# A transformer in one kernel: gate products of the second block in three passes of high and low parts, their weights split by GpSimd

## The chip, the cores and the metric

The kernel runs on one core of one Trainium2 chip. The metric is the device time of one execution in microseconds, the median of three runs. A core has TensorE (PE, matrix products into eight banks of accumulators), VectorE (DVE), ScalarE (ACT), GpSimd (POOL) and SyncE (SP, which here only issues transfers).

## The reference, cut to what matters

The input of 256 tokens by 1024 goes through two blocks of two layers each, all in float32. The second block, the one that matters here, has in each of its two layers a mixer:

```
p_swa, p_rwkv, p_fox, p_dsa, p_gate = split_cols(x @ w_in, IN_GROUPS)
o_swa, o_rwkv, o_fox, o_dsa = (four branches: two kinds of attention, a recurrent
                               one in chunks, and attention over the top keys)
gates = sigmoid(p_gate.reshape(B, S, 4, 1024) + gate_bias)
merged = zeros_like(x)
for i, (o, w) in enumerate(zip((o_swa, o_rwkv, o_fox, o_dsa), w_rows)):
    merged = merged + gates[:, :, i] * (o @ w)
y = merged @ w_out
x = layer_norm(ALPHA * x + y, ln_g, ln_b)
```

then a feed-forward part (dense in the first layer, eight experts with two picked per token in the second) and another layer norm. The gate projection p_gate is x (256 by 1024) times 1024 by 4096: in tiles of 128 by 128 weights it is 32 output tiles (four branches, eight column tiles) of eight products each, 256 gate blocks a layer.

## The kernel before, in words

Activations lie with their features on the partitions and the tokens in the free dimension, so a product takes a 128x128 tile of weights against 256 tokens. All weights come as one stream of chunks; a chunk is four such tiles side by side, 128x512 float32. SP loads chunk n into slot n % 11 of `ring` (line 747) and waits, before it overwrites a slot, until the chunk that lay there is used up (`slot_left`, lines 725 to 732).

A projection or feed-forward product is made in three passes: weights and activations are each kept as a high part, rounded to the narrower matrix format (fp32r), and a low part, the rest. ScalarE rounds a chunk from `ring` into `WH` (`high_to`, issued through line 1746), VectorE subtracts it into `WL` (`low_to`, line 2525); both buffers have six slots (SPLIT). PE then multiplies high by high, high by low and low by high (lines 853, 856 and 857, in `split_tile`). A slot may be rounded into again once PE has begun the chunk after the slot's last user (`split_begun`).

Two kinds of chunks aren't split but read by PE from `ring` as plain float32: in the mixer the gate weights (`gates`, line 1167, against X) and the branch weights (`branches`, through `mm`, line 815, against the branch outputs in A). The stream has them block by block in the order in which the mixer uses them (`mixer_fill`, lines 174 to 206), so a chunk may hold both kinds.

The mixer's order is written out by hand, and every engine follows its own list. PE's list sets gate products as filler between the small products of the branches: so many blocks in each attention step (four), after the index scores (eight), between steps of the recurrent branch, one or two at each scan step, and 21 at the end. In front of a product that needs VectorE's results PE waits: `ready_wait` for VectorE's `go()`, which is a tiny memset (line 2223). Gate tiles go alternately to banks 6 and 7; ScalarE takes each with a tanh (line 1746, out to A), VectorE multiplies it with the branch product and adds it into the merged sum, which lies in the second half of X (lines 2506, 2509, 2511).

The first half of X holds the layer's input x in float32. It is read by the gate products, and at the mixer's end by the residual addition. After the first layer's feed-forward part ScalarE writes it back eight tiles at a time (`x_written(6)`, called at line 1809). Beside it the same x lies as high and low parts in PH and PL, for the projections. GpSimd has no work.

## Time and profile before

| what | us |
|---|---|
| median of three runs | 2484.52 (2483.64 to 2503.65) |
| span of the profiled execution | 2475.0 |
| PE / DVE / ACT / POOL busy | 2381.7 / 1527.2 / 1090.0 / 0.2 |
| gate products (line 1167), 1024 records | 249.4 busy |
| the mixer's stretch of one layer | 1118 to 1336, and 1650 to 1868 |

The profiled execution's own time is its span, 2475.0 us, which runs from its first to its last instruction; the time of a run includes what lies around that, and the median is 9.5 us longer. Busy times of matmuls overlap and their ends are modelled, so PE at 96% isn't PE at its peak. A float32 product leaves two matmul records, one of a split pass leaves one. Idle time of an engine is shown before the instruction that ended it, with what released it. The second block's two mixers lie at the two stretches above and look alike.

### The profile page before, as it was taken

The numbers are of one execution on the slowest core, as the hardware profiler recorded it, in microseconds if no ns is written. First come the engines' busy times: TensorE is split into PE (matmuls) and PEld (weight loads), VectorE is DVE, ScalarE is ACT, GpSimd is POOL, SyncE is SP. The second block draws the span as 40 slices with busy tenths as digits, with TensorE's granted clock in tenths as the row PEclk, the third lists the DMA queues.
The fourth block names the chain that finished last, engine by engine and source line by source line (L and its number), as shares of the span: only waits on it lengthen the run. The fifth ranks groups of instructions, "written<-read, shape, count | busy, mean of one in ns | idle before, by whom it ended". The sixth has DMA issues, their size and how long they took to land.

```text
span 2475.0 us, 41012 instructions
## 1 busy us (share of the span) xinstructions
PE 2381.7 (96%) x15617; PEld 1977.1 (80%) x15617; DVE 1527.2 (62%) x3424; ACT 1090.0 (44%) x2009; POOL 0.2 (0%) x4
## 2 busy tenths in 40 slices
PE   7998999999998999999999899999998999999998
PEld 3853688888884899997788899997787888778885
DVE  4567453333477776766566766856747655558893
ACT  3236343222335665543303545542304444557881
POOL 0000000000000000000000000000000000000000
PEclk9999999999999999999999999999999999999999
DMA  9237423333325666653334466543332755459997
GB/s 336 90 118 256 154 85 94 102 92 96 94 86 186 206 186 188 193 177 90 93 100 130 151 196 194 167 127 96 107 85 70 256 190 174 141 204 354 333 357 269
DMA packets 182499, 409.85 MB, mean 166 GB/s; under 512 B 20256, under 2 KB 20512, under 8 KB 181792
## 3 DMA queue, kind: packets, MB, share of 16 engines
q1 hardware_dynamic: 182304, 407.23, 50.4%
q8 instruction: 125, 2.05, 0.3%
q14 instruction: 70, 0.57, 0.1%
HBM read 406.10 MB, written 1.05 MB: 165 GB/s over the span
## 4 chain that ended last, share of the span: by engine, by line
PE 88%; DVE 8%; ACT 1%; issue 1%; DMA 1%; SPq 0%; DVEq 0%; ACTq 0%
PE bank L853 11%; PE bank L856 11%; PE bank L857 11%; PE bank L1167 9%; PE bank L1184 6%; PE bank L1187 5%; PE bank L1188 5%; PE bank L815 5%; PE bank L873 2%; PE bank L876 2%; PE bank L877 2%; PE bank L1008 2%; PE bank L1094 2%; PE bank L1142 2%; PE bank L1319 1%
## 5 line engine op out<-in xcount | busy, mean ns | idle before, releaser
L2525 DVE TENSOR_TENSOR WL<-ring,WH 128x512 fp32r<-128x512 f32 x632 | 413.4, 686 | 228.5 <-ACT WH L1746 226.8
L1746 ACT ACTIVATE WH<-ring 128x512 fp32r<-128x512 f32 x632 | 375.9, 625 | 286.4 <-PE bank L853 196.6
L2610 DVE TENSOR_TENSOR WLE<-slots,WHE 128x1024 fp32r<-128x1024 f32 x231 | 281.2, 1223 | 123.0 <-ACT WHE L1746 119.9
L1746 ACT ACTIVATE WHE<-slots 128x1024 fp32r<-128x1024 f32 x231 | 244.7, 1061 | 115.0 <-PE bank L1184 113.7
L853 PE MATMUL bank<-AH,WH 128*128 128x256 f32 (+1 forms) x832 | 266.0, 320 | 10.1 <-DVE WL L2525 4.6
L856 PE MATMUL bank<-AL,WH 128*128 128x256 f32 (+1 forms) x832 | 265.4, 319 | 0.0
L857 PE MATMUL bank<-AH,WL 128*128 128x256 f32 (+1 forms) x832 | 263.7, 317 | 0.0
L1167 PE MATMUL bank<-X,ring 128*128 128x256 f32 x1024 | 249.4, 391 | 0.0
L1167 PEld LDWEIGHTS bank<-X,ring 128*128 128x128 f32 x1024 | 189.4, 191 | 35.6 <-issue 7.3
L853 PEld LDWEIGHTS bank<-AH,WH 128*128 128x128 f32 x832 | 157.8, 190 | 24.5 <-DVE WL L2525 5.0
L857 PEld LDWEIGHTS bank<-AH,WL 128*128 128x128 f32 x832 | 157.7, 190 | 12.1
L856 PE MATMUL bank<-HL,WH 128*128 128x256 f32 (+1 forms) x528 | 166.6, 315 | 0.0
L856 PEld LDWEIGHTS bank<-AL,WH 128*128 128x128 f32 x832 | 157.8, 190 | 10.7
L853 PE MATMUL bank<-HH,WH 128*128 128x256 f32 (+1 forms) x528 | 166.2, 315 | 0.0
L857 PE MATMUL bank<-HH,WL 128*128 128x256 f32 (+1 forms) x528 | 165.5, 314 | 0.0
L1184 PE MATMUL bank<-WHE,XEH 128*128 128x512 f32 (+1 forms) x432 | 164.2, 380 | 0.2 <-DVE WLE L2610 0.2
L1188 PE MATMUL bank<-WLE,XEH 128*128 128x512 f32 (+1 forms) x432 | 161.0, 373 | 0.0
L1187 PE MATMUL bank<-WHE,XEL 128*128 128x512 f32 (+1 forms) x432 | 160.8, 372 | 0.0
L853 PE MATMUL bank<-PH,WH 128*128 128x256 f32 (+2 forms) x416 | 129.3, 311 | 5.1 <-DVE PL L2323 2.8
L857 PE MATMUL bank<-PH,WL 128*128 128x256 f32 (+2 forms) x416 | 126.4, 304 | 0.0
L1746 ACT ACTIVATE A<-bank,par 128x256 f32<-128x256 f32 x60 | 28.3, 471 | 197.5 <-PE bank L1167 168.8
L856 PE MATMUL bank<-PL,WH 128*128 128x256 f32 (+2 forms) x384 | 113.5, 296 | 0.0
(419 smaller groups left out, 4790.5 us busy)
## 6 DMA issues: line engine op xcount, KB each, us to landing
ring<-stream SPq DMA_DIRECT2D x992, 256.0 KB, 2.8
slots<-experts SPq DMA_DIRECT2D x264, 512.0 KB, 5.3
con<-consts SPq DMA_DIRECT2D x1, 2884.0 KB, 13.1
X<-xin SPq DMA_DIRECT2D x1, 2048.0 KB, 10.3
par<-params SPq DMA_DIRECT2D x1, 1302.5 KB, 6.7
LAST<-final_rows SPq DMA_DIRECT2D x1, 1024.0 KB, 4.9
out<-ZO SPq DMA_DIRECT2D x4, 256.0 KB, 2.0
con<-consts SPq DMA_DIRECT2D x1, 132.0 KB, 2.7
```

What stands on the lines that cost most here:

```text
L815: ins = pe.matmul(o, l, r, start=start, stop=stop)
L853: ins = pe.matmul(o, wh, hi(kk), start=kk == 0, stop=False)
L856: read_signal(pe.matmul(o, wh, lo(kk), start=False, stop=False))
L857: ins = pe.matmul(o, wl, hi(kk), start=False, stop=kk == k - 1)
L873: ins = pe.matmul(o, wh, hi(kk, tt), start=kk == 0, stop=False)
L1167: ins = pe.matmul(o, weight(st["n"]), X[:, kk, 0:T], start=kk == 0, stop=kk == KD - 1)
L1184: ins = pe.matmul(o, hi, WHE[:, s, at:at + w], start=start, stop=False)
L1187: pe.matmul(o, lo, WHE[:, s, at:at + w], start=False, stop=False)
L1188: return pe.matmul(o, hi, WLE[:, s, at:at + w], start=False, stop=stop)
L1746: return nc.scalar.activation(o, i, fn, **kw)
L2525: V.tensor_tensor(WL[:, s % SPLIT, :], ring[:, c % RING, :], WH[:, s % SPLIT, :].bitcast(F32), ALU.subtract).then_inc(w_taken, 1)
L2610: V.tensor_tensor(WLE[:, s % PAIR_SPLIT, :], pair(pair_of(s)), WHE[:, s % PAIR_SPLIT, :].bitcast(F32), ALU.subtract).then_inc(pair_taken, 1)
```

## The change: what it does

- `gates` makes three passes (`wh` by high x, `wh` by low x, `wl` by high x) instead of one float32 product.
- GpSimd gets a list of work: per layer it copies x's low parts out of PL (`X_LOW`, partly laid over constants no longer used, and `X_LOW_MORE`), x's high parts out of PH into X's own place (`XR`), then splits the gate chunks (copy into `WH`, subtraction into `WL`, one high ahead of each low), and at the end adds high and low back into X. It waits for the loaded chunk and for `split_begun`.
- Gate chunks and branch chunks are separate now (`mixer_chunks`): a gate chunk holds four gate blocks, a branch chunk the tiles of one or two branch products. SP waits for GpSimd's split (`gate_taken`) before it overwrites a gate chunk, and for PE's read before it overwrites a branch chunk.
- The gate chunks take their turn in the six split slots; the counts that PE and VectorE wait for leave them out.
- `x_written(6)` is gone; VectorE waits for `x_back` before the output projection's residual additions.

```diff
@@ -90,6 +90,8 @@
 
 PO, NPAR = offsets(PARAM_COLS)
 CO, NCON = offsets(CONST_COLS)
+X_LOW_AT, X_LOW_TILES = 944, 5
+assert CO["cos"][0] <= X_LOW_AT and X_LOW_AT + X_LOW_TILES * T <= CO["band"][1]
...
@@ -203,6 +205,20 @@
     branch(KD)
     assert sum(n for kind, n in order if kind == "gate") == len(PAIRS) * KD
     assert sum(n for kind, n in order if kind == "branch") == len(PAIRS)
+    return order
+
+
+def mixer_chunks():
+
+    order, wanted, gate_chunks_, pairs_ = [], dict(gate=0, branch=0), 0, 0
+    for kind, n in mixer_fill():
+        wanted[kind] += n
+        while kind == "gate" and CHUNK * gate_chunks_ < wanted["gate"]:
+            order.append(("gate", gate_chunks_, 1))
+            gate_chunks_ += 1
+        while kind == "branch" and pairs_ < wanted["branch"]:
+            order.append(("branch", pairs_, CHUNK // BR_K[PAIRS[pairs_][0]]))
+            pairs_ += order[-1][2]
     return order
...
@@ -291,16 +307,13 @@
             blocks.append((w, (l,), kk * P, (C_DSA + 320, C_DSA + 704), (64, 4)))
         wide(w, (l,), C_FOX + 512, 2)
         gates = [(i, j, kk) for i, j in PAIRS for kk in range(KD)]
-        branches = list(PAIRS)
-        for kind, n in mixer_fill():
+        for kind, first, count in mixer_chunks():
             if kind == "gate":
-                for i, j, kk in gates[:n]:
+                for i, j, kk in gates[CHUNK * first:CHUNK * (first + 1)]:
                     blocks.append((w, (l,), kk * P, C_GATE + i * D + j * P, P))
-                gates = gates[n:]
             else:
-                for i, j in branches[:n]:
+                for i, j in PAIRS[first:first + count]:
                     tiles("w_branch_2", (l,), [j * P], BR_K[i], sum(BR_K[:i]) * P)
-                branches = branches[n:]
         pad()
         projections.append(len(blocks) // CHUNK)
         outward("w_out_2", (l,))
...
@@ -348,6 +361,9 @@
         with ExitStack() as rounding:
             rounding.enter_context(nc.sbuf_tensor("under_rounded", [P, (RING + 2 * SPLIT) * CHUNK * P], F32))
             XR = rounding.enter_context(nc.sbuf_tensor("XR", [P, KD, TT], F32R))
+        with ExitStack() as second:
+            second.enter_context(nc.sbuf_tensor("under_x_low", [P, (RING + 2 * SPLIT) * CHUNK * P + KD * TT + NPAR + X_LOW_AT], F32))
+            X_LOW = second.enter_context(nc.sbuf_tensor("X_LOW", [P, X_LOW_TILES, T], F32R))
         slots = sb("slots", RING + 2 * SPLIT, CHUNK * P)
         X = sb("X", KD, TT)
         par = sb("par", NPAR)
...
@@ -444,6 +461,14 @@
 
         def small(at, n):
             return smalls[:, at:at + n]
+
+        def x_high(j):
+
+            return XR[:, j, 0:T]
+
+        def x_low(j):
+
+            return X_LOW[:, j, :] if j < X_LOW_TILES else X_LOW_MORE[:, j - X_LOW_TILES, :]
 
         def early_gain(ni):
 
...
@@ -727,9 +754,12 @@
                 if whole(n):
 
                     sp.wait_ge(w_read, read_count(n) + 1)
+                elif gate_chunk(n):
+
+                    sp.wait_ge(gate_taken, gates_before(n) + 1)
                 else:
 
-                    sp.wait_ge(w_taken, split_index(n) + 1)
+                    sp.wait_ge(w_taken, split_index(n) - gates_before(n) + 1)
 
             first_par, first_con = slice(0, FIRST_PAR), slice(0, FIRST_CON)
             sp.dma_start(par[:, first_par], params[:, first_par]).then_inc(cond_in, 16)
...
@@ -848,7 +878,7 @@
                     first = n % CHUNK == 0
                     if first:
 
-                        pe.wait_ge(w_taken, s + 1)
+                        pe.wait_ge(w_taken, s - st["gated"] + 1)
                     wh, wl = (W[:, s % SPLIT, c][:, 0:o.shape[0]] for W in (WH, WL))
                     ins = pe.matmul(o, wh, hi(kk), start=kk == 0, stop=False)
                     if first:
...
@@ -1161,22 +1191,45 @@
 
                 for _ in range(n):
                     g, kk = divmod(st["gate"], KD)
+                    at = st["gate"] // CHUNK
+                    slot, c = split_index(GATES_OF_ALL[at]) % SPLIT, st["gate"] % CHUNK
                     if kk == 0 and g >= 2:
                         pe.wait_ge(gate_kept, g - 1)
+                    if g % len(PAIRS) == 0:
+                        pe.wait_ge(x_highs, KD * (g // len(PAIRS)) + kk + 1)
+                    if c == 0:
+                        pe.wait_ge(gate_taken, at + 1)
                     o = bank[6 + g % 2][:, 0:T]
-                    ins = pe.matmul(o, weight(st["n"]), X[:, kk, 0:T], start=kk == 0, stop=kk == KD - 1)
+                    wh, wl = (W[:, slot, c * P:(c + 1) * P] for W in (WH, WL))
+                    ins = pe.matmul(o, wh, x_high(kk), start=kk == 0, stop=False)
+                    if c == 0:
+                        ins.then_inc(split_begun, 1)
+                    read_signal(pe.matmul(o, wh, x_low(kk), start=False, stop=False))
+                    ins = pe.matmul(o, wl, x_high(kk), start=False, stop=kk == KD - 1)
                     if kk == KD - 1:
                         ins.then_inc(gate_mm, 1)
-                    else:
-                        read_signal(ins)
-                    st["n"] += 1
                     st["gate"] += 1
 
             def branches(n):
 
-                for i, j in PAIRS[st["p"]:st["p"] + n]:
-                    tile(lambda kk: CAT2[:, sum(BR_K[:i]) + kk, :], BR_K[i], T)
+                for p in range(st["p"], st["p"] + n):
+                    i, j = PAIRS[p]
+                    chunk, at, last = branch_place(st["layer"], p)
+                    b = unit_begin()
+                    if at == 0:
+                        pe.wait_ge(w_loaded[chunk % RING], 16 * (chunk // RING + 1))
+                    for kk in range(BR_K[i]):
+                        mm(b[:, 0:T], ring[:, chunk % RING, (at + kk) * P:(at + kk + 1) * P], CAT2[:, sum(BR_K[:i]) + kk, :],
+                           kk == 0, kk == BR_K[i] - 1, kk == BR_K[i] - 1)
+                    if last:
+                        st["free"] += 1
                 st["p"] += n
+
+            def mixed(l):
+
+                st["gated"] += len(GATE_AT[l])
+                st["n"], st["s"] = CHUNK * PROJ_START[5 + 2 * l], split_index(PROJ_START[5 + 2 * l])
+                st["layer"] += 1
 
             def passes(p, at, w, o, hi, lo, start, stop, begins):
 
...
@@ -1194,7 +1247,7 @@
                 pe.matmul(bank[5][:, 0:P], ONES[:, :], BEFORE[:, :], start=True, stop=True).then_inc(slot_mm, 1)
                 rw = pr("router_w").rearrange("p (k e) -> p k e", k=KD)
                 for kk in range(KD):
-                    pe.wait_ge(n_out, 2 * KD + kk + 1)
+                    pe.wait_ge(n_out, KD + kk + 1)
                     ins = pe.matmul(bank[6][0:EXPERTS, 0:T], rw[:, kk, :], X[:, kk, 0:T], start=kk == 0, stop=kk == KD - 1)
                 ins.then_inc(router_mm, 1)
 
...
@@ -1728,8 +1781,7 @@
 
 
                 branches(KD)
-                skip_to_chunk()
-                whole_end()
+                mixed(l)
                 out_projection(PLN, CLN, T, 5 + 2 * l)
                 if l == 0:
                     ffn(2, T, 6, early=5)
@@ -1805,8 +1857,6 @@
                     if j % 2:
                         high_to(after + 10 + j // 2)
                 high_to(after + 14)
-                if ni >= 6:
-                    x_written(ni, bias)
 
             def norm_root(ni, tt, eps):
 
...
@@ -2521,7 +2571,7 @@
 
                 while st["c"] < min(upto, CHUNKS):
                     c, s = st["c"], split_index(st["c"])
-                    dve.wait_ge(w_hi, s + 1)
+                    dve.wait_ge(w_hi, s - gates_before(c) + 1)
                     V.tensor_tensor(WL[:, s % SPLIT, :], ring[:, c % RING, :], WH[:, s % SPLIT, :].bitcast(F32),
                                     ALU.subtract).then_inc(w_taken, 1)
                     st["c"] += 1
@@ -3186,9 +3236,9 @@
                 for j in (KD - 2, KD - 1):
                     merged_low(l, j)
                 if l:
-                    dve.wait_ge(n_out, 2 * KD)
                     V.tensor_scalar(BEFORE[:, :], cn("causal", 0, P), NEG / 2, None, ALU.is_lt).then_inc(route_tables, 1)
                     V.memset(ONES[:, :], 1.0).then_inc(route_tables, 1)
+                dve.wait_ge(x_back, KD * (l + 1))
                 projections(5 + 2 * l, [(X[:, j, 0:T], grouped(j), lambda d, b, j=j: residual_parts(j, b, T, ALPHA))
                                         for j in range(KD)], 16 + AHEAD, 5 + 2 * l, T)
                 settled()
@@ -3208,6 +3258,45 @@
                            PROJ_START[6] + AHEAD, early_hidden_tiles(range(2)), [SQ_[:, j, :] for j in range(GROUP)])
 
 
+        @block.gpsimd
+        def _(pool):
+            G = nc.gpsimd
+
+            def gate_high(g):
+
+                c = GATES_OF_ALL[g]
+                at = split_index(c)
+                pool.wait_ge(w_loaded[c % RING], 16 * (c // RING + 1))
+                pool.wait_ge(split_begun, at - SPLIT + 2)
+                G.tensor_copy(WH[:, at % SPLIT, :], ring[:, c % RING, :]).then_inc(gate_hi, 1)
+
+            def gate_low(g):
+
+                c = GATES_OF_ALL[g]
+                slot = split_index(c) % SPLIT
+                pool.wait_ge(gate_hi, g + 1)
+                G.tensor_tensor(WL[:, slot, :], ring[:, c % RING, :], WH[:, slot, :].bitcast(F32),
+                                ALU.subtract).then_inc(gate_taken, 1)
+
+            for l in range(2):
+                first, end = len(GATE_AT[0]) * l, len(GATE_AT[0]) * (l + 1)
+                pool.wait_ge(a_lo, KD * (7 + 3 * l))
+                for j in range(KD):
+                    G.tensor_copy(x_low(j), PLN[:, j, :]).then_inc(x_lows, 1)
+                for j in range(KD):
+                    G.tensor_copy(x_high(j), PHN[:, j, :]).then_inc(x_highs, 1)
+                for g in range(first, end):
+                    gate_high(g)
+                    if g > first:
+                        gate_low(g - 1)
+                gate_low(end - 1)
+                pool.wait_ge(gate_mm, len(PAIRS) * (l + 1))
+                pool.wait_ge(x_lows, KD * (l + 1))
+                pool.wait_ge(x_highs, KD * (l + 1))
+                for j in range(KD):
+                    G.tensor_tensor(X[:, j, 0:T], x_high(j).bitcast(F32), x_low(j).bitcast(F32), ALU.add).then_inc(x_back, 1)
+
+
 IDLE = {1: (4, 1, 5), 2: (4, 1, 5), 7: (2, 1, 4)}
 
 
...
@@ -3274,17 +3363,36 @@
 CHUNKS = FIRST_EXPERT
 IN_CHUNKS = 54
 WHOLE = [(0, PROJ_START[0]), (PROJ_START[0] + 40, PROJ_START[1]), (PROJ_START[2] + 24, PROJ_START[3])]
-WHOLE += [(PROJ_START[4 + 2 * _l] + IN_CHUNKS, PROJ_START[5 + 2 * _l]) for _l in range(2)]
+GATE_AT = [[PROJ_START[4 + 2 * _l] + IN_CHUNKS + _n for _n, _x in enumerate(mixer_chunks()) if _x[0] == "gate"]
+           for _l in range(2)]
+BRANCH_AT = [[PROJ_START[4 + 2 * _l] + IN_CHUNKS + _n for _n, _x in enumerate(mixer_chunks()) if _x[0] == "branch"]
+             for _l in range(2)]
+BRANCH_PAIRS = [_x for _x in mixer_chunks() if _x[0] == "branch"]
+GATES_OF_ALL, BRANCHES_OF_ALL = GATE_AT[0] + GATE_AT[1], BRANCH_AT[0] + BRANCH_AT[1]
+
+
+def gate_chunk(c):
+
+    return c in GATES_OF_ALL
 
 
 def whole(c):
 
-    return any(lo <= c < hi for lo, hi in WHOLE)
+    return any(lo <= c < hi for lo, hi in WHOLE) or c in BRANCHES_OF_ALL
 
 
 def read_count(c):
 
+    if c in BRANCHES_OF_ALL:
+        return sum(hi - lo + 1 for lo, hi in WHOLE) + BRANCHES_OF_ALL.index(c)
     return sum(min(c + 1, hi) - lo + (c >= hi) for lo, hi in WHOLE if lo <= c)
+
+
+def branch_place(l, p):
+
+    n = next(n for n, (_, first, count) in enumerate(BRANCH_PAIRS) if first <= p < first + count)
+    _, first, count = BRANCH_PAIRS[n]
+    return BRANCH_AT[l][n], (p - first) * BR_K[PAIRS[p][0]], p == first + count - 1
 
 
 HALF_STEPS = {3: range(0, 4), 7: range(4, 8), 11: range(8, 12), 15: range(12, 16), 19: range(16, 20), 21: (20, 21),
@@ -3428,7 +3536,12 @@
 
 def split_index(c):
 
-    return c - sum(hi - lo for lo, hi in WHOLE if lo < c)
+    return c - sum(hi - lo for lo, hi in WHOLE if lo < c) - sum(b < c for b in BRANCHES_OF_ALL)
+
+
+def gates_before(c):
+
+    return sum(g < c for g in GATES_OF_ALL)
 
 
 
```

(The other places of the diff change `w_taken, s + 1` into `w_taken, s - st["gated"] + 1` in the same way.)

## Rows read from the trace of the kernel before

**Rows 1.** The page, part 1: busy us (share of the span) and instructions of each engine.

```profile
PE 2381.7 (96%) x15617; PEld 1977.1 (80%) x15617; DVE 1527.2 (62%) x3424; ACT 1090.0 (44%) x2009; POOL 0.2 (0%) x4
```

**Rows 2.** Line 1167 by itself: count, ns min/median/max, first and last start; busy tenths.

```profile
L1167 PE MATMUL bank<-X,ring x1024: 377/379/635, 1118.4 to 1867.5; 128*128 128x256 f32 x171
...
busy tenths in 40 slices 0000000000000000009999000059994000000000
```

**Rows 3.** Windows: stretch, length, busy us (instructions) of each engine, granted clock, DMA.

```profile
1118.00:1336.00 218.00, 215.34 (x1788) 173.74 (x1787) 137.93 (x465) 57.72 (x148) 0.00 (x0) 0.99 0.34 96
1650.00:1868.00 218.00, 215.34 (x1790) 173.71 (x1790) 137.93 (x465) 57.37 (x147) 0.00 (x0) 0.99 0.33 95
...
1153.00:1180.00 27.00, 25.52 (x130) 21.16 (x129) 24.25 (x90) 1.42 (x3) 0.00 (x0) 1.00 0.45 130
1229.00:1256.00 27.00, 26.21 (x210) 21.50 (x209) 25.73 (x47) 8.97 (x13) 0.00 (x0) 1.00 0.34 97
```

**Rows 4.** The chain that ended last: start us, us, what; one run of gate products.

```profile
1221.83 6.91 PE bank L1167 x32
```

**Rows 5.** Timeline of PE in the projections: start, us, instruction.

```profile
1059.85 0.28 PE L853 MATMUL bank<-PH,WH 128*128 128x256 f32 x1
...
1063.25 0.28 PE L853 MATMUL bank<-PH,WH 128*128 128x256 f32 x1
```

**Rows 6.** Timeline of VectorE: attention steps, five marks and later.

```profile
1144.64 0.29 DVE L2460 COPY A<-bank 128x128 f32<-128x128 f32 x1 [0.51 <-PE bank L1142]
1145.25 0.42 DVE L2480 CUSTOM_DVE_ANT_0 S<-bank,con 128x256 f32<-128x256 f32 x1 [0.32 <-PE bank L1094]
...
1148.00 0.29 DVE L2460 COPY A<-bank 128x128 f32<-128x128 f32 x1 [0.24 <-PE bank L1142]
...
1226.92 0.06 DVE L2223 MEMSET smalls<- 128x1 f32 x1
...
1245.45 0.06 DVE L2223 MEMSET smalls<- 128x1 f32 x1
...
1267.08 0.06 DVE L2223 MEMSET smalls<- 128x1 f32 x1
...
1334.51 0.06 DVE L2223 MEMSET smalls<- 128x1 f32 x1
...
1349.64 0.69 DVE L2525 TENSOR_TENSOR WL<-ring,WH 128x512 fp32r<-128x512 f32 x1 [1.52 <-ACT WH L1746]
```

**Rows 7.** Timeline of PE: the units behind VectorE's results.

```profile
1165.52 1.99 PE L815 MATMUL bank<-A,ring 128*128 128x256 f32 x8 [0.69 <-DVE X L2506]
...
1180.00 0.49 PE L1094 MATMUL bank<-S 64*128 64x128 f32 x4 [0.40 <-DVE X L2506]
...
1228.57 1.02 PE L815 MATMUL bank<-S,con 128*128 128x512 f32 x2
...
1245.64 1.91 PE L1621 MATMUL bank<-con,S 128*128 128x128 f32 x16
...
1268.28 1.15 PE L815 MATMUL bank<-S 64*64 64x64 f32 x32
...
1335.40 7.07 PE L815 MATMUL bank<-A,ring 128*128 128x256 f32 x32
```

**Rows 8.** The page, part 5: weight splits on VectorE and ScalarE; busy, mean ns, idle before.

```profile
L2525 DVE TENSOR_TENSOR WL<-ring,WH 128x512 fp32r<-128x512 f32 x632 | 413.4, 686 | 228.5 <-ACT WH L1746 226.8
L1746 ACT ACTIVATE WH<-ring 128x512 fp32r<-128x512 f32 x632 | 375.9, 625 | 286.4 <-PE bank L853 196.6
```

**Rows 9.** Groups of VectorE's instructions, 1118 to 1336, shapes apart.

```profile
L2511 DVE TENSOR_TENSOR X<-X,A 128x256 f32<-128x256 f32 x16 | 6.8, 425 | 0.5
...
L3063 DVE RECIPROCAL S<-S 128x512 f32<-128x512 f32 x1 | 3.3, 3342 | 0.0
```

**Rows 10.** The instructions on tile WH: ns min/median/max of VectorE's subtraction.

```profile
L2525 DVE TENSOR_TENSOR WL<-ring,WH x632: 624/684/694, 36.1 to 1891.7; 128x512 fp32r<-128x512 f32 x158
```

**Rows 11.** Timeline of ScalarE in the second layer's projections: one weight copy of many.

```profile
1619.80 0.63 ACT L1746 ACTIVATE WH<-ring 128x512 fp32r<-128x512 f32 x1 [0.73 <-PE bank L853]
```

13 lines of the change are left out of this document (8 added, 5 removed).

## The prediction, made before the changed kernel had run

> **What bounds the kernel now.** The page comes first: PE is busy 96% of the span, VectorE 62%, ScalarE 44%, GpSimd four instructions [rows 1]. A busy share says only where to look, since matmul records overlap. Then line 1167 by itself: the gate products lie in two stretches, one per layer of the second block [rows 2]. The windows of those stretches show 215.3 us of PE work in 218 us, twice the same: PE paces the mixer as a whole, with VectorE at 138 us beside it [rows 3]. The smaller windows show where that isn't so: in two stretches of 27 us a layer VectorE has hardly a gap (24.25 and 25.73 us busy), and PE's gate products are only filler there [rows 3].
>
> **What a gate block costs before and after.** A gate block is one 128x128 weight tile against 256 tokens. In f32 it leaves two matmul records, so the 1024 records of line 1167 are 512 blocks, 256 a layer. An undisturbed run of 32 records takes 6.91 us on the chain, 0.216 us a record, 0.432 us a block [rows 4]. The three passes are in this trace already, in the projections: the first pass of a block starts at 1059.85 and that of the tenth block after it at 1063.25, which is 0.340 us a block [rows 5]. Their shape, operand kinds and weight loads (188 ns, overlapped) are those of the new gate products. PE saves 0.092 us a block, 23.6 us a layer, 47.1 us in all.
>
> [...]
>
> **What of it reaches the end.** PE is in order, so a shorter gate run pays until the next instruction has to wait for VectorE. I read the end of each "go" mark of VectorE, the small memset of line 2223 [rows 6], against the start of PE's next unit [rows 7].
> - Attention steps: in two steps (6.5 us) VectorE idles 0.51, 0.32 and 0.24 us, waiting for PE [rows 6]; the cut is 0.74 us. All is kept here, and in the second attention, where VectorE's pauses are longer still.
> - Index scores, 1153 to 1180: PE waits already (0.69 and 0.40 us for line 2506). 20 blocks, 1.8 us: lost.
> - 1229 to 1245.6: the mark ends at 1245.51, PE's next unit starts at 1245.64. 24 blocks, 2.2 us, with 0.13 us to spare: 2.1 us lost.
> - The run of 16 blocks from 1221.67 covers a mark that ends at 1226.98, PE going on at 1228.57: 1.6 us to spare, cut 1.5. Kept.
> - Level steps: a mark ends at 1267.14 and PE needs it at 1268.28, behind gates and a branch product: 1.1 us to spare, cut 0.37. Kept.
> - Last run, 21 blocks: the mark ends at 1334.57, PE goes on at 1335.40. Of 1.9 us, 0.8 is kept and 1.1 lost. Late next is VectorE's normalisation behind it.
> The rest, the scan with its small gate runs, has pauses over what is cut. Lost: 5.0 us a layer; kept: 18.6 us; both layers 37.2 us.
>
> **GpSimd's new work.** Per layer 64 chunks, each a 128x512 copy and a 128x512 subtraction. No row shows GpSimd at such work. The nearest rows are ScalarE's copy, 625 ns, and VectorE's subtraction, 686 ns, of the same tiles [rows 8]: 1.31 us a chunk, 84 us a layer. That is the value I take, as the nearest, and the low end (a quicker chunk would be hidden as well and change nothing). The far end is a copy at the price of the trace's slowest 128x512 instruction, VectorE's reciprocal, with the subtraction: 3.34 + 0.69 = 4.0 us a chunk [rows 9]. PE will ask for a chunk every 1.36 us within a run, but only every 3.1 us on average (218 - 18.6 = 199.4 us over 64), and six split slots stand between them. At 1.31 us it is hidden by that spacing; without it every microsecond would be PE's wait. The longest runs, 32 blocks from 1319.8 on, ask for 8 chunks in about 13 us, of which six may be ready: hidden up to some 6 us a chunk there. ScalarE and VectorE split no gate chunk before or after, so nothing is taken from them.
>
> The Trainium skill (GPSIMD Engine Reference, Performance versus the Vector engine) gives 2.6 cycles an element for a two-input instruction and 769 ns for a tight 512-element loop; by it a chunk would be estimated at some 1.9 us, still under 3.1, and the sum would be the same.
>
> **GpSimd beside VectorE.** This is the disputed term: does a busy GpSimd slow VectorE? Below, 0: VectorE's 686 ns subtraction runs next to a busy ScalarE and takes 624 to 694 ns everywhere [rows 10]. Above, where VectorE paces (54 us a layer) all of GpSimd's time comes on top: 20 blocks and about 29 more are 12 chunks, at 1.31 us 15.7 us a layer. A gain is excluded: nothing leaves VectorE. I take 6 us a layer, 12 in all: the nearest row says zero, but ScalarE isn't GpSimd, and in those stretches VectorE has no gap to absorb anything; so a good third of the upper end.
>
> **The small edits.** At the start GpSimd makes x's two parts, 16 copies of 128x256; by ScalarE's and VectorE's rows for that size, 0.4 us each, under 8 us. It waits for the last low part of the layer's input, and PE is at full-rate projections with them by 1060, 58 us before the first gate product at 1118.4 [rows 5, 2]: hidden by the projections; without that cover 7 us. Its first gate chunk must wait until PE has begun a chunk five before, about 7 us ahead, enough for four or five chunks. At the end it rebuilds X, 8 additions of 128x256 at 425 ns [rows 9], 3.4 us after the last gate product at 1335.4; behind VectorE's new wait stand the weight subtractions of the output projection and the residual additions, and VectorE takes up the first of them at 1349.64 [rows 6]. Hidden; even at three times the price 4 us before it is needed. ScalarE loses 8 writes of X, about 3 us, while it idles 0.73 us before each weight copy [rows 11]: 0. The SP queue waits for GpSimd's split where it waited for PE's read, up to six chunks earlier: 0, or a gain in slack. Branch products read the same chunks at the same price. The stream keeps its 84 chunks. The granted clock is 0.99 over the mixer [rows 3], which leaves no term.
>
> **Sum.** 37.2 saved, 12 given back: 25.2 us. The profiled execution's span of 2475.0 becomes 2450; the median of the runs is 9.5 us more, 2484.5, which becomes **2459 us**.
>
> **Rivals.**
> *The two engines don't touch each other.* For it: ScalarE and VectorE together. Time 2484.5 - 37.2 = 2447. Chance 0.22.
> *They exclude each other, and GpSimd is quick.* VectorE pays 15.7 us where it paces; and in the attention steps two chunks (2.6 us) fall in two steps that have 1.07 - 0.74 = 0.33 us left; with half of it in the way 1.0 us is lost, four times. 19.7 us against the 18.6 kept: 2487, no change. Against it: no row. The Trainium skill (SBUF — State Buffer, the section on the shared port) says that a VectorE instruction with two SBUF inputs, or in a two-port mode, and a GpSimd instruction that reads SBUF lock each other out fully; VectorE's chain at 1229 to 1256 is mostly of such instructions. This trace, where GpSimd does nothing, can't show it. Chance 0.25.
> *Slower: GpSimd sets the pace of the gates.* It decides when a chunk costs it over 218/64 = 3.4 us with all its delays. If a chunk takes twice the rows, 2.6 us (168 us a layer), and it stands still for half of VectorE's 138 us, a layer takes 237 us: 19 us more, 2523 in all. For it: two instructions a chunk in order on one engine, with a semaphore between. Against: the rows' 1.31 us leave a factor of 2.6. At the far end of 4.0 us a chunk, 256 us a layer, it would be 2560; I leave that outside the range. Chance 0.20.
> *The passes don't run at 0.113 us.* Nothing speaks for it [rows 5], and I give it nothing of its own. The forecast keeps 0.33; its own range is 2450 to 2471.
>
> **How the numbers follow.** What a measurement here can tell from no change is about 1%, 25 us, so faster means below 2460, and the forecast sits on that border. That is the first rival and half of the forecast, 0.38; within 1%: the other half and the second rival, 0.41; slower 0.21 (the third and a little for what is not on the list). Range: 2440 (a little beyond the first rival) to 2525 (the third).
>
> **What would show it.** Per block 0.34 us in line 1167's successors, three records each; GpSimd's start-to-start spacing within a chunk against 1.3 and 3.1 us; VectorE's 128x512 subtraction at 686 ns, or longer beside GpSimd; PE's wait for GpSimd before a gate's first pass (none expected); PE waits of about 2 us before 1245 and 1 us at the last mark; the mixer's 218 us down to about 205. A mixer over 218 us, or GpSimd named as PE's releaser, proves it wrong.

## The result and the profile after

The changed kernel takes **2517.35 us** (median of 4 runs, 2508.69 to 2530.25) beside 2485.55 us for the kernel before on the same chip: a ratio of 1.012 (95% interval 1.0092 to 1.0149), 32 us slower. The forecast was 2459, 25 us faster. The profiled execution took 2516.61 us, its span is 2514.7 us.

Those two are 1.9 us apart. So the 9.5 us between the median before and its profiled span aren't only what surrounds a span: the execution that was profiled before was some 7.6 us quicker than the median. Its granted clock was 0.988; 67 other executions of that kernel had 0.982 to 0.988 and took 2478.9 to 2501.5 us. Its first mixer begins at 1118.2 us, in the thirteen other traces at 1122.0 to 1130.6. I therefore compare stretches between the same instructions, and not whole spans.

Part 1 of the page, busy us by engine, against [rows 1]; and the costliest groups of part 5 for the gate products and the weight splitting.

```profile
PE 2379.5 (95%) x16129; PEld 1996.2 (79%) x16129; DVE 1590.4 (63%) x3424; ACT 1086.6 (43%) x2001; POOL 282.6 (11%) x308
...
L3278 POOL TENSOR_TENSOR WL<-ring,WH 128x512 fp32r<-128x512 f32 x128 | 170.4, 1332 | 0.0
L2575 DVE TENSOR_TENSOR WL<-ring,WH 128x512 fp32r<-128x512 f32 x632 | 416.1, 690 | 232.4 <-ACT WH L1798 230.6
L1204 PE MATMUL bank<-XR,WH 128*128 128x256 f32 x512 | 161.9, 316 | 9.0 <-ACT A L1798 9.0
```

The last row is the first of three passes, one record for each of the 512 blocks, where [rows 2] had two records a block. GpSimd's work is there: 128 subtractions of 1.33 us. VectorE executes the same 3424 instructions as before, and is busy longer with them. The rest of GpSimd's work, from the groups of its engine:

```profile
L3271 POOL CAST WH<-ring 128x512 fp32r<-128x512 f32 x128 | 86.8, 678 | 299.3 <-PE bank L1204 178.6 <-PE bank L1012 94.7 <-DMA ring<-stream 25.7
L3297 POOL TENSOR_TENSOR X<-XR,X_LOW 128x256 f32<-128x256 f32 x10 | 9.4, 970 | 11.7 <-PE bank L1208 11.7
```

A chunk is 0.68 + 1.33 = 2.01 us. Between its chunks GpSimd waited mostly for TensorE (line 1204, 178.6 us): it was ahead. TensorE's waits name GpSimd as releaser for 0.5 us in the whole run.

The first mixer, which was 218.00 us in [rows 3], as a window of its own:

```profile
1126.00:1352.00 226.00, 206.42 (x2040) 177.68 (x2039) 165.83 (x464) 56.81 (x147) 119.49 (x122) 0.95 0.30 93
```

TensorE has 9 us less to do than before (206.4 for 215.3) and 20 us of gaps; VectorE has 464 instructions, one less than in that window, but 165.8 us for 137.9. TensorE's longest waits in that window (what waited, for whom; us in all, times, longest):

```profile
PE bank L845 <- DVE smalls L2273: 6.0, 3, 5.0
PE bank L1204 <- ACT A L1798: 4.5, 1, 4.5
PE bank L1157 <- DVE S L2500: 3.1, 2, 1.7
```

The memset of line 2273 is VectorE's go mark, which was line 2223. ScalarE, the releaser in the second row, had itself waited for VectorE, 7.64 us for line 3121 and then 1.93 us for line 2561. So the time is lost to a slow VectorE, and the question is what slowed it.

For a comparison by stage I take the starts of the same VectorE instructions in each trace: the first mixer in four stages, which begin at 1118.23, 1181.16, 1222.02 and 1263.54 of the trace before and end at 1357.11. These are the last three of the changed kernel (columns: window, its us, then busy us and instructions of PE, PEld, DVE, ACT, POOL, granted clock, DMA share, GB/s):

```profile
1190.70:1232.56 41.86, 41.47 (x279) 35.04 (x278) 21.93 (x89) 14.62 (x46) 20.54 (x22) 0.84 0.19 62
1232.56:1285.79 53.23, 41.27 (x360) 35.59 (x360) 49.01 (x74) 12.74 (x19) 30.06 (x28) 0.90 0.29 95
1285.79:1375.62 89.83, 85.18 (x1133) 76.90 (x1134) 60.23 (x140) 20.92 (x40) 41.98 (x44) 1.00 0.37 116
```

In the same instructions the kernel before needs 40.9, 41.5 and 93.6 us. The middle row is VectorE's own stretch: busy 49.01 of 53.23 us. A layer's 256 gate blocks lie in the four stages as 68, 45, 56 and 87.

### The profile page after: what moved, and what is told of

Same layout as the page of the kernel before. It is cut to its first block, busy times and chain, and to the rows that moved or that the text cites. A ratio compares the mean times of both kernels' runs of the same rounds, so it can differ in the third digit from the quotient of the medians.

```text
span 2514.7 us, 42477 instructions
## 1 busy us (share of the span) xinstructions
PE 2379.5 (95%) x16129; PEld 1996.2 (79%) x16129; DVE 1590.4 (63%) x3424; ACT 1086.6 (43%) x2001; POOL 282.6 (11%) x308
## 4 chain that ended last, share of the span: by engine, by line
PE 81%; DVE 14%; issue 2%; ACT 2%; DMA 1%; SPq 0%; DVEq 0%; ACTq 0%
PE bank L887 11%; PE bank L886 11%; PE bank L883 11%; PE bank L1237 6%; PE bank L1240 5%; PE bank L1241 5%; PE bank L845 4%; PE bank L903 2%; PE bank L1204 2%; PE bank L906 2%; PE bank L907 2%; PE bank L1038 2%; PE bank L1124 2%; DMA ring<-stream 1%; PE bank L1372 1%
## 5 line engine op out<-in xcount | busy, mean ns | idle before, releaser
L3278 POOL TENSOR_TENSOR WL<-ring,WH 128x512 fp32r<-128x512 f32 x128 | 170.4, 1332 | 0.0
L1204 PE MATMUL bank<-XR,WH 128*128 128x256 f32 x512 | 161.9, 316 | 9.0 <-ACT A L1798 9.0
L3285 POOL CAST X_LOW<-PL 128x256 fp32r<-128x256 f32 x10 | 6.8, 721 | 1319.2 <-DVE PL L2371 1065.5
L1208 PE MATMUL bank<-XR,WL 128*128 128x256 f32 x512 | 147.8, 289 | 0.0
## 6 DMA issues: line engine op xcount, KB each, us to landing
con<-consts SPq DMA_DIRECT2D x1, 2884.0 KB, 13.7
```

Of the source, the lines that this page charges most:

```text
L1204: ins = pe.matmul(o, wh, x_high(kk), start=kk == 0, stop=False)
L1208: ins = pe.matmul(o, wl, x_high(kk), start=False, stop=kk == KD - 1)
L3278: G.tensor_tensor(WL[:, slot, :], ring[:, c % RING, :], WH[:, slot, :].bitcast(F32), ALU.subtract).then_inc(gate_taken, 1)
```

## The experiments

All kernels are the changed one with the edits shown, which are shortened here; times are medians, and each ratio is to the kernel before, run on the same chip (2484.8 to 2486.5 us on the chips used). **Theory A** to begin with: GpSimd's work holds VectorE up. Its rival: GpSimd's chunks, or the passes themselves, cost TensorE time. Where GpSimd works on one column, the other 511 keep what lay there, so these kernels leave out most of the gate weights' split.

**GpSimd's work taken away, its order kept.**

```
-  G.tensor_copy(WH[:, at % SPLIT, :], ring[:, c % RING, :])
+  G.tensor_copy(WH[:, at % SPLIT, 0:1], ring[:, c % RING, 0:1])
-  G.tensor_tensor(WL[:, slot, :], ring[:, c % RING, :], WH[:, slot, :].bitcast(F32), ALU.subtract)
+  G.tensor_tensor(WL[:, slot, 0:1], ring[:, c % RING, 0:1], WH[:, slot, 0:1].bitcast(F32), ALU.subtract)
```

> The changed kernel with every GpSimd weight split cut to one column of 512 (128 copies and 128 subtractions remain, with all their waits; the gate values are not the reference's). Theory A, GpSimd's full-width splits lock VectorE's two-input and fast SBUF instructions out: VectorE's line 3090 (3040 before) falls back from 1149 to 478 ns, its work in a mixer from 180 to about 150 us, and the time falls to 2484.5 - 37 = about 2447, the sum of the prediction without contention. Rival B, the loss comes from the three passes themselves (more records, GpSimd's queue and its semaphores, the copies of x): the time stays above 2500. Rival C, the clock alone, lower after short gate runs: half-speed time stays near 124 us in the span and the time near 2500.

Measured: 2470.6 us, ratio 0.9926 (0.9897 to 0.9955). GpSimd's elements cost 47 us. But 2470.6 is not 2447: of 37 us that the passes were to bring, only 15 came. Two questions, then: how GpSimd costs 47 us, and where 22 us of gain went.

**The passes taken away, GpSimd whole.**

```
-  (the three products wh by x_high, wh by x_low, wl by x_high)
+  pe.matmul(o, wh.bitcast(F32), x_high(kk).bitcast(F32), start=kk == 0, stop=kk == KD - 1)
```

> The changed kernel with GpSimd's splits whole, but PE makes one float32 product per gate block from the split buffers in place of three passes (it leaves out the low part of weights and of x). PE's work is that of before, GpSimd's that of after. Theory A: VectorE's extra 30 us a mixer stays, since GpSimd does the same; PE gives no 23.6 us a layer back, but where VectorE paces that costs nothing, so some 2484.5 + 2 x (13 in the recurrent branch's preparation + 3 elsewhere) = about 2515 to 2540. Rival B (the passes are to blame): 2485 to 2490.

Measured: 2536.9 us, ratio 1.0188 (1.0154 to 1.0222). With TensorE's work as before the change, GpSimd's alone makes the kernel 51 us slower. The passes are no part of the loss.

**One of GpSimd's two instructions whole, the other at one column**, in each of two kernels.

> The changed kernel with GpSimd's copies whole (678 ns each, one SBUF input) and its subtractions cut to one column: about a third of GpSimd's time at the shared port stays. Theory A, an exclusive lock for as long as the GpSimd instruction runs: VectorE's extra in a mixer about 10 us of the 30, longest single delay under 0.7 us, time about 2460. Rival D, only GpSimd's two-input instructions disturb VectorE: extra 0, time 2447.

> The changed kernel with GpSimd's subtractions whole (1332 ns each, two SBUF inputs) and its copies cut to one column: two thirds of GpSimd's time at the port. Theory A: VectorE's extra about 20 us a mixer, longest single delay about 1.1 us, time about 2485. Rival D: extra as in the changed kernel, 30 us, time about 2500.

Measured: copies 2481.9 us (0.9979, 0.9961 to 0.9997), subtractions 2509.1 us (1.0083, 1.0054 to 1.0112). Over the one-column kernel that is 11 and 38 us, together 50: they add up to about the 47, and the subtraction is three quarters of it, with two thirds of the busy time. Neither forecast of times came true (2460 and 2485 by theory A, 2447 and 2500 by rival D). The longest delay of a single VectorE instruction is 0.42 us beside the copies (678 ns each) and 1.14 us beside the subtractions (1332 ns), less than one GpSimd instruction each time, as theory A has it; and since the copies delay at all, rival D falls.

What it does to VectorE is seen best between the one-column and the changed kernel, whose lines are the same. VectorE's groups over the first mixer, one-column kernel (busy us, mean ns of one):

```profile
L2559 DVE SCALAR_TENSOR_TENSOR A<-A,bank 128x256 f32<-128x256 f32 x22 | 9.2, 416 | 10.6 <-PE bank L845 10.4
...
L3074 DVE MAX8 smalls<-S 128x8 f32<-128x128 f32 (+1 forms) x16 | 5.8, 362 | 0.4
...
L2498 DVE RECIPROCAL smalls<-smalls 128x1 f32<-128x1 f32 x32 | 5.1, 159 | 0.7
...
L3090 DVE SCALAR_TENSOR_TENSOR S<-S,par 128x256 f32<-128x256 f32 x8 | 3.3, 481 | 0.0
...
L2497 DVE TENSOR_TENSOR smalls<-smalls 128x1 f32<-128x1 f32 x16 | 2.4, 151 | 0.3 <-ACT smalls L1798 0.3
```

and the changed kernel:

```profile
L2559 DVE SCALAR_TENSOR_TENSOR A<-A,bank 128x256 f32<-128x256 f32 x22 | 9.2, 416 | 10.4 <-PE bank L845 10.2
L3090 DVE SCALAR_TENSOR_TENSOR S<-S,par 128x256 f32<-128x256 f32 x8 | 8.7, 1149 | 0.0
L2497 DVE TENSOR_TENSOR smalls<-smalls 128x1 f32<-128x1 f32 x16 | 8.7, 541 | 1.2 <-ACT smalls L1798 1.2
...
L3074 DVE MAX8 smalls<-S 128x8 f32<-128x128 f32 (+1 forms) x16 | 5.8, 361 | 0.4
...
L2498 DVE RECIPROCAL smalls<-smalls 128x1 f32<-128x1 f32 x32 | 5.1, 159 | 0.7
```

A 151 ns addition of two 128x1 columns becomes 541 ns, a 481 ns instruction 1149. The one that reads a PSUM bank stays at 416 ns, MAX8 and the reciprocal don't move. In the first mixer of the kernel before VectorE's instructions sum to 150.4 us, in the one-column kernel to 150.7, with copies alone to 156.4, with subtractions alone to 176.8, with both to 180.1. Instruction by instruction over the four stages, the extra is 29.8 us, and it lies in 192 instructions of four kinds with all operands in SBUF: TENSOR_TENSOR (mean 502 to 681 ns), TENSOR_SCALAR (262 to 357), SCALAR_TENSOR_TENSOR (492 to 759) and TENSOR_TENSOR_SCAN (679 to 1113). The same kinds with an operand in PSUM (`bank`) keep their times within 1 ns, and MAX8, MATCH_REPLACE8 and RECIPROCAL theirs. The rule is the one in the Trainium skill (SBUF — State Buffer, Who interferes with whom): a VectorE instruction with two SBUF inputs contends with a GpSimd instruction that reads SBUF, and whichever came first keeps the port for its whole length. The trace agrees: in this kernel that small addition never took over 1218 ns, the wait being less than one 1332 ns subtraction of GpSimd. What short GpSimd instructions in a row do is another matter, and comes below.

The same chain of VectorE instructions in VectorE's timeline, in the one-column kernel (start, us, then the instruction):

```profile
1238.73 3.34 DVE L3113 RECIPROCAL S<-S 128x512 f32<-128x512 f32 x1
1242.11 0.69 DVE L3114 TENSOR_TENSOR S<-S 128x512 f32<-128x512 f32 x1
1242.83 0.43 DVE L3117 TENSOR_SCALAR S<-S 128x512 f32<-128x512 f32 x1
1243.29 1.27 DVE L3119 TENSOR_TENSOR_SCAN S<-con,S 128x256 f32<-128x256 f32 x2
1244.60 0.69 DVE L3121 TENSOR_TENSOR S<-S 128x512 f32<-128x512 f32 x1
1245.21 0.61 DVE L3123 TENSOR_SCALAR S<-S,par 128x256 f32<-128x256 f32 x2
```

and in the changed kernel, with GpSimd's timeline beside it:

```profile
1249.46 3.34 DVE L3113 RECIPROCAL S<-S 128x512 f32<-128x512 f32 x1
1252.84 0.75 DVE L3114 TENSOR_TENSOR S<-S 128x512 f32<-128x512 f32 x1
1253.62 0.72 DVE L3117 TENSOR_SCALAR S<-S 128x512 f32<-128x512 f32 x1
1254.37 2.59 DVE L3119 TENSOR_TENSOR_SCAN S<-con,S 128x256 f32<-128x256 f32 x2
1256.99 1.60 DVE L3121 TENSOR_TENSOR S<-S 128x512 f32<-128x512 f32 x1
1258.52 1.97 DVE L3123 TENSOR_SCALAR S<-S,par 128x256 f32<-128x256 f32 x2
```
```profile
1254.02 1.44 POOL L3278 TENSOR_TENSOR WL<-ring,WH 128x512 fp32r<-128x512 f32 x1
1255.72 0.69 POOL L3271 CAST WH<-ring 128x512 fp32r<-128x512 f32 x1 [0.26 <-PE bank L1204]
1256.38 1.66 POOL L3278 TENSOR_TENSOR WL<-ring,WH 128x512 fp32r<-128x512 f32 x1
1258.00 1.07 POOL L3271 CAST WH<-ring 128x512 fp32r<-128x512 f32 x1
```

From the second row on, seven instructions of 3.69 us take 7.63 us, with no gap between them; the scans and what follows them wait 0.6 to 0.9 us each. The reciprocal takes 3.34 us in both.

**Where does GpSimd's work cost?** Two kernels in which GpSimd works whole on some chunks and on one column of the rest:

```
+  few = CHUNK * P if 28 <= g % 64 < 38 else 1      (the other kernel: if g % 64 >= 38)
-  [..., :]   in both instructions
+  [..., 0:few]
```

> GpSimd splits in full only the ten gate chunks 28 to 37 of each mixer (those that TensorE reads from about 1222 to 1262, where VectorE's chain sets the pace), the other 54 in one column each, so that most gates are computed from wrong halves. Theory A, GpSimd's work costs time only where VectorE sets the pace: this stretch alone lengthened by 14 us in mixer 1 and 17 us in mixer 2 between the one-column kernel and the changed one, so about 30 of the 47 us are back with 10 of 64 chunks: 2498 to 2503. Theory B, the cost is in proportion to GpSimd's work: 10/64 of 47 us is 7, 2478.

> The other way round: GpSimd splits in full only the 26 gate chunks 38 to 63 of each mixer (levels, scan and tail, about 1262 to 1336), the first 38 in one column each. Theory A, GpSimd's work costs only where VectorE sets the pace: in this stretch TensorE does, the VectorE instructions are stretched all the same, and the time stays within 3 us of the one-column kernel's 2470.6: 2471 to 2474. Theory B, cost in proportion to the work: 26/64 of 47 us is 19, 2490.

Measured: 2486.2 us (1.0, 0.9976 to 1.0023) and 2480.1 us (0.9988, 0.9967 to 1.001). Ten chunks cost 15.6 us over the one-column kernel (in proportion 7), 26 chunks 9.5 us (in proportion 19). Neither number of theory A was right, but the place is: 1.6 us for each of the ten chunks, 0.4 us for each of the late ones. The late chunks first, the third and the fourth stage of that kernel's first mixer:

```profile
1221.35:1265.96 44.61, 38.86 (x360) 34.78 (x360) 40.92 (x74) 12.74 (x19) 20.70 (x28) 0.92 0.35 113
1265.96:1356.30 90.34, 86.38 (x1134) 78.28 (x1135) 60.57 (x141) 21.01 (x40) 42.22 (x45) 0.98 0.39 117
```

and the same two stages of the one-column kernel:

```profile
1229.08:1268.21 39.13, 36.48 (x360) 32.46 (x360) 35.17 (x74) 12.76 (x19) 8.44 (x30) 1.00 0.37 129
1268.21:1357.72 89.51, 86.02 (x1134) 78.24 (x1135) 56.86 (x140) 21.05 (x40) 13.14 (x41) 0.98 0.38 119
```

In the fourth stage GpSimd is busy 42 us and the stage is 0.8 us longer. The cost, 5.5 us, is in the third: GpSimd works up to six split slots ahead of TensorE, so it split the "late" chunks while VectorE's chain was running. I had left that out, and had set the border too early as well: TensorE comes to chunk 38 at 1253.9 us of the trace before, within the third stage, not at 1262. With 7.3 us for the ten chunks in the same stage (46.47 less 39.13 in that kernel) this gives 12.8 us, and between the one-column and the changed kernel the stage grows by 53.23 - 39.13 = 14.1.

**Is the clock the rest?** The missing gain, first. The stages by kernel, in us, and behind the slash how many of them TensorE's clock stood at half; both mixers:

```
stage (start before)  1118.2     1181.2     1222.0     1263.5   | 1650.6     1714.2     1755.4     1795.9
before                62.9/ 0.0  40.9/ 3.4  41.5/ 0.0  93.6/0.0 | 63.6/ 0.0  41.1/ 3.4  40.5/ 0.0  94.5/0.0
one column            59.3/ 0.0  41.9/13.7  39.1/ 0.0  89.5/3.4 | 60.0/ 0.0  42.2/13.7  38.1/ 0.0  91.5/3.4
changed               64.6/ 0.0  41.9/13.7  53.2/10.2  89.8/0.0 | 65.5/ 1.3  46.3/19.1  51.0/13.7  90.7/0.0
one column, filled    59.3/ 0.0  40.3/10.2  39.1/ 0.0  89.5/3.4 | 59.9/ 0.0  40.7/10.2  38.1/ 0.0  91.5/3.4
changed, filled       66.7/ 0.0  45.0/20.5  50.8/ 0.0  90.2/3.4 | 66.3/ 1.3  46.3/19.2  48.5/ 0.0  92.3/3.4
late chunks whole     59.3/ 0.0  38.8/ 6.8  44.6/ 6.8  90.3/3.4 | 59.9/ 0.0  42.3/13.7  43.6/ 6.8  91.2/0.0
late split (first)    63.0/ 0.0  40.9/ 3.4  45.0/ 3.4  87.7/0.0 | 63.6/ 0.0  39.5/ 0.0  45.3/ 6.8  88.8/0.0
late split (last)     63.0/ 0.0  42.5/ 6.8  41.5/ 0.0  87.8/0.0 | 63.6/ 0.0  39.5/ 0.0  40.5/ 0.0  89.1/0.0
```

Half is a granted share of 0.5, the lower of TensorE's two levels (1.2 and 2.4 GHz). The second stage, where gate products alternate with score products, didn't get shorter in three passes: the clock was at half for 13.7 us there and not for 3.4. Where that time is the same, the passes do bring what was expected of them: with 6.8 us at half the stage is 38.8 us in three passes (late chunks whole) and 42.5 us in one product (last late split). Two kernels put idle products into TensorE's waits, three and three at the index scores in both, and in the changed kernel eleven, ten and four more behind them:

```
+  def fill(n):
+      b = bank[st["u"] % BANKS]
+      if st["u"] >= BANKS:
+          pe.wait_ge(gemm_free, st["u"] - BANKS + 1)
+      for _ in range(n):
+          pe.matmul(b[:, 0:T], ident, cn("chunks", 0, T), start=True, stop=True)
```

> The one-column kernel (GpSimd's copies and subtractions of gate weights cut to one column of 512, so the gates are computed from wrong halves) with six idle TensorE products of 128x256 in float32 (0.432 us each) in each mixer: three before the branch product that waited 1.22 us (1170.33 to 1171.55), three before the scores that waited 1.34 us (1184.70 to 1186.04). In that kernel TensorE's clock stood at half for 13.7 us of mixer 1 right behind these waits, 3.4 us in the kernel before. Theory A, the clock fell because TensorE stood still: with the waits filled it is at half for about 3.4 us again, 10.2 us of half speed less in each mixer, some 5 us each: 2470.6 becomes about 2460. Theory B, the clock falls for the three-pass products themselves or by chance: the half-speed time stays near 13.7 us and the time at 2470 to 2473.

> The changed kernel whole, with idle TensorE products in each mixer's waits: six in the index scores as in the kernel just before this, eleven in the 4.96 us wait at 1238.03, ten in the 4.45 us wait at 1258.30, four in the 1.74 us wait at 1267.38. They change nothing that GpSimd and VectorE do. Theory A, the waits pull the clock down behind them, and that is a part of the 47 us between this kernel with and without GpSimd's work: half-speed time in mixer 1 falls from 23.9 us to 3 to 10 us, and the time from 2517 to between 2500 and 2508. Theory B, the waits alone cost and the clock is no part: 2515 to 2520, or more for products that overrun a wait.

Measured: 2461.6 us (0.9897, 0.9853 to 0.9941) and 2509.6 us (1.0092, 1.0063 to 1.0121), 9 and 8 us under the kernels without fillers. For the changed kernel that is just above theory A's 2500 to 2508, but its half-speed time in the first mixer stayed at 23.9 us, where 3 to 10 were expected. The stage rows bear theory A out in the third stage alone: no half-speed time for 10.2 us, and 50.8 for 53.2 us, in the second mixer 48.5 for 51.0; so of the 14.1 us some 2.4 are clock, lost behind TensorE's own waits, the rest VectorE. The second stage got worse (45.0 us, 20.5 of them at half speed, for 41.9 and 13.7). The two mixers together are 3.0 us longer in this trace, of an execution 7.6 us over its median. Over all executions the granted clock rose, from 0.970 to 0.976 in the changed kernel to 0.975 to 0.980 with fillers; in which stages, the one trace can't say.

For the one-column kernel the time came close to theory A's 2460, but the trace doesn't carry it: half-speed time fell from 13.7 to 10.2 us only, and the mixers became 1.6 us shorter each. 5 us of the difference between the traces lie ahead of the first mixer, in code that is the same. The windows of the same instructions, first the one-column kernel and then the filled one:

```profile
936.67:1127.89 191.22, 190.16 (x1619) 189.06 (x1618) 118.40 (x234) 93.69 (x175) 10.85 (x25) 1.00 0.58 179
937.24:1122.78 185.54, 184.48 (x1618) 183.39 (x1618) 118.15 (x235) 93.45 (x175) 10.83 (x25) 1.00 0.60 185
```

TensorE alone takes 3% longer, with a granted clock of 1.00 in both, and VectorE and ScalarE take the same. The changed kernel's trace has such a stretch between its mixers (174.67 us for the one-column kernel's 168.88), so it isn't a matter of the fillers. The short waits at the index scores held at most a quarter of the half-speed time, and that expectation's mechanism falls.

**Shorter GpSimd instructions.**

```
-  one copy and one subtraction of 512 columns
+  for q in range(4): the same on columns q * P to (q + 1) * P
```

> The changed kernel whole, but each GpSimd copy and each GpSimd subtraction of a gate chunk is four instructions of 128 columns in place of one of 512. Theory A, a VectorE instruction that meets GpSimd's stands still until that instruction of GpSimd ends: the longest of VectorE's small 149 ns subtractions, 1218 ns in the changed kernel, falls to about 0.5 us and their mean from 541 ns to 250 or less; VectorE's sum in mixer 1 falls from 180 us to about 165, and the time from 2517 to 2495 to 2505. Theory B, the two share the way to memory by the element, and what counts is GpSimd's total: VectorE's sum stays at 180 us or grows with GpSimd's, and the time is 2515 to 2530.

Measured: 2511.4 us, ratio 1.0102 (1.0083 to 1.012), between the two theories. The small addition of line 2497 (the expectation calls it a subtraction) has these durations now (ns, shortest, median, longest):

```profile
L2497 DVE TENSOR_TENSOR smalls<-smalls x16: 150/270/1155, 1138.8 to 1160.9; 128x1 f32<-128x1 f32 x16
```

for 148/601/1218 in the changed kernel: more often short (mean 340 ns for 541), at worst nearly as long, where theory A had 500. And other instructions waited longer than ever:

```profile
L3127 DVE TENSOR_TENSOR S<-S 128x512 f32<-128x512 f32 x1 | 2.4, 2448 | 0.0
...
L3038 DVE TENSOR_SCALAR smalls<-par 128x8 f32<-128x8 f32 x1 | 2.3, 2298 | 0.0
```

They are 0.68 and 0.16 us before the change. The wait of 1.8 to 2.1 us is as long as four subtraction pieces in a row, or longer (1.74 us by GpSimd's timeline): a train of short instructions keeps VectorE out as a long one does, where a wait for the one instruction that came first would have ended after some 0.5 us. VectorE's sum over the mixer falls from 180.1 to 172.6 us, GpSimd's grows from 128.6 to 190 us a layer.

**A version for keeping.** Split only late chunks, compute the others as one float32 product from the ring as before the change; X stays whole, so nothing is rebuilt. First with 26 chunks, then with 20 and GpSimd held back, then with 22 and ScalarE's copies moved:

```
+  PLAIN = range(0, 38)        then range(0, 44), then range(0, 42)
+  if not gate_chunk(chunk):
+      ins = pe.matmul(o, ring[:, chunk % RING, c * P:(c + 1) * P], X[:, kk, 0:T], start=kk == 0, stop=kk == KD - 1)
+  for j in range(KD): f(x_high(j), X[:, j, 0:T], ACT.Copy)      (ScalarE, into free scratch)
+  pool.wait_ge(gate_mm, len(PAIRS) * l + 20)                    (second and third kernel)
```

> A version meant to be kept. Only the 26 gate chunks 38 to 63 of each mixer (levels, scan and tail, from 1262 on, where TensorE sets the pace) are split by GpSimd and computed in three passes; the first 38 are one float32 product a block from the ring, as before the change. X stays whole in float32, its low part is copied by GpSimd as in the change, its high part by ScalarE after attention into scratch that is free by then, and nothing is rebuilt. By the trace of the one-column kernel 26 chunks save 9.6 us a mixer less 1.1 at the end; GpSimd works six slots ahead, and so meets VectorE's chain between 1229 and 1256: by e8 5.5 us a mixer. Theory A (cost by place): 9.6 - 1.1 - 5.5 = 3 us a mixer, about 2480 beside 2486 before. Theory B (cost in proportion to GpSimd's work, 26 of 64 chunks): 8.5 - 9.5 = -1 a mixer, 2488.

> The same, with only the 20 gate chunks 44 to 63 split, and GpSimd held until TensorE has finished the twentieth gate product of the mixer (about 1262), behind VectorE's chain. 20 chunks x 4 blocks x 0.092 = 7.4 us a mixer, less 1.1 at the end and 0.9 for the stretched VectorE instructions between 1262 and 1336. Theory A (GpSimd costs only where VectorE sets the pace): 5.4 us a mixer, 2475 beside 2486 before, and the stretch 1229 to 1256 as long as before the change (26.6 us). Theory B (in proportion, 20 of 64 chunks of 47 us over two mixers): 6.3 - 7.3 = -1 a mixer, 2488.

> The version with late splitting (g2) with two edits: ScalarE copies X's high part 6 us earlier, in its idle stretch before VectorE's first mark of the third part (in g2 it lay between two of VectorE's marks, and the stretch from 1222 to 1262 was 42.5 us in place of 41.5 in mixer 1 and 41.5 in place of 40.5 in mixer 2), and 22 chunks, 42 to 63, are split in place of 20. Theory A (GpSimd costs only where VectorE sets the pace): 1 us for the copies and 2 x 0.368 = 0.7 us for the chunks, in each mixer: 3.4 us under g2's 2482.0, 2478 to 2479, a ratio of 0.996 to 0.998 to the kernel before. Theory B (in proportion to GpSimd's work): the two chunks bring nothing or cost 0.7 us a mixer: 2480 to 2484.

Measured: 2485.8 us (ratio 0.9998, 0.998 to 1.0016), 2482.0 us (0.9981, 0.9962 to 1.0001), and **2473.9 us** (0.9947, 0.9928 to 0.9966). The last one beats both kernels: 11 us under the one before, 43 under the changed one. The first two are 6 and 7 us over theory A's 2480 and 2475. The first gained 5.9 us in its fourth stage and lost 3.5 in the third, to the chunks that GpSimd splits there again. The second, with six chunks fewer and GpSimd held back, lost 1.0 there; which of the two edits did it was not separated. The last one's third and fourth stage:

```profile
1230.45:1271.90 41.45, 40.65 (x305) 33.56 (x305) 35.24 (x74) 12.76 (x20) 5.86 (x7) 1.00 0.40 114
1271.90:1359.73 87.83, 85.21 (x1133) 76.94 (x1134) 57.97 (x141) 20.90 (x40) 36.05 (x38) 1.00 0.40 125
```

The third is as long as before the change (41.5), with 35.24 us of VectorE, as there. In the fourth GpSimd is busy 36 us, and the stage is 5.7 us shorter than before. It did better than theory A's 2478: in the traces the two mixers are 4.2 and 7.1 us shorter than before, 11.2 in all, which is what the medians say. From the second version to the third, though, the medians fall by 8.1 us and the traces' mixers by 3.0, near the 3.4 expected; where the other 5 us lie no trace shows.

## Why the prediction was wrong

By its own steps:

- **A block goes from 0.432 to 0.340 us: too good.** The three passes take 0.354 us. From the last gate run of the changed kernel's first mixer, a first pass and that of the tenth block after it, at a granted clock of 1.00:

```profile
1346.11 0.28 PE L1204 MATMUL bank<-XR,WH 128*128 128x256 f32 x1
1349.65 0.28 PE L1204 MATMUL bank<-XR,WH 128*128 128x256 f32 x1
```

  That is a pass every 0.118 us, where [rows 5] had 0.113. In all twelve kernels with such blocks the median is 0.353 to 0.360 us in each stage, and the float32 block stays at 0.432. So TensorE is spared 0.078 us a block and not 0.092, 20.0 us a layer for 23.6. The step that failed is that the projections' spacing was taken for the gates'; why it differs is open.
- **What reaches the end, 18.6 us a mixer: twice what came.** The one-column kernel saves 9.1 and 8.0 us. By stage the prediction had 4.5, 4.1, 3.1 and 6.9 us; mixer one gave 3.6, -1.0, 2.4 and 4.1. The slower passes take 2.8 us of the 18.6 (202 blocks kept). Two entries failed besides. *The clock as no term*: in the second stage, over both mixers of four kernels each, it was at half for 11.9 us on average with three passes and GpSimd's chunks hardly in the way (one column, one column filled, ten chunks, late chunks), and for 3.0 us with one product (before, and the three versions for keeping), and the stage took 41.5 and 40.8 us: what the passes saved there the clock took. The row that I read, 0.99 over the mixer, was of the kernel whose products were to be replaced. *The rebuild of X as hidden*: in the fourth stage the changed kernel needs 89.8 and 90.7 us, the first late-split version, with the same 26 chunks split, the clock as full and no rebuild, 87.7 and 88.8: 2 us a mixer. GpSimd's additions take 0.97 us, not 0.43 [rows 9]. Nobody waits for them: they end at 1359.6, and the first residual addition comes at 1373.85. But they hold up VectorE beside them, on whose work TensorE waits next:

```profile
1352.01 4.69 POOL L3297 TENSOR_TENSOR X<-XR,X_LOW 128x256 f32<-128x256 f32 x5 [5.85 <-PE bank L1208]
```
```profile
1354.26 0.97 DVE L2561 TENSOR_TENSOR X<-X,A 128x256 f32<-128x256 f32 x1
1356.03 1.21 DVE L2575 TENSOR_TENSOR WL<-ring,WH 128x512 fp32r<-128x512 f32 x1
1358.04 0.95 DVE L2567 SCALAR_TENSOR_TENSOR CL<-X,PL 128x256 fp32r<-128x256 f32 x1
```

  Undisturbed these take 0.42, 0.69 and 0.42 us. From VectorE's last mark to the first residual addition it is 21.3 us here and 19.3 in the late-split version. Together the three account for the 9.5 us missing in the first mixer, as an estimate: 2.8 for the spacing, 4.5 for the clock (in the second stage 45 blocks at 0.078 us are 3.5 us, and it gave -1.0) and 2 for the rebuild.
- **A GpSimd chunk at 1.31 us: 2.01 measured**, between the ends; as predicted it made no difference by itself. The 1.9 us worked out from the Trainium skill (GPSIMD Engine Reference, Performance versus the Vector engine) was nearer than my rows, which were of other engines.
- **GpSimd beside VectorE, 6 us a mixer: this step turned the sign.** It measures 19.6 us in the first mixer and 21.7 in the second, over even the upper end of 15.7; with the 37.2 us as predicted the kernel would still have come out slower. The end left out three things: a chunk is 2.01 us and not 1.31, which alone makes the same sum 24 us; a stretched instruction is one that *waits*, so a 0.15 us instruction can lose over a microsecond, and in the first stage that made TensorE wait where VectorE had pauses (5.2 us); and the clock falls behind TensorE's new waits (2.4 us). My middle value had leaned on ScalarE's row next to VectorE [rows 10], which speaks for another engine.
- **Small edits:** the x copies at the start, the SP queue and ScalarE's lighter load show in no wait of TensorE's in the mixers. VectorE's 128x512 subtraction of weights stayed at 690 ns, since it hardly ever runs in the gates' part beside GpSimd's: as a witness it was badly chosen.

*The rivals.* That the two exclude each other was the right mechanism, and its 2487 came 30 us short, by the sizes above. "Slower" by GpSimd setting the pace gave 2523, near the result, for a reason that didn't occur: TensorE waited 0.5 us for it. That the result lies within the range of 2440 to 2525, whose upper end comes from this rival, is therefore luck. By the prediction's own test, a mixer over 218 us, it was readable from one row (226).

**Open:** why the clock falls more often in the second stage when gate products are three passes. Fillers in the waits ahead of it took away a quarter of the half-speed time and no more; whether fillers among the score products would take more was not tried. Open too is why a pass is placed every 0.118 us in the mixers, at a granted clock of 1.00, and every 0.113 in most projections.
